# Top-k threshold search: 12 bits on VectorE and 20 on ScalarE, in place of 16 and 16

## What is computed

```python
dots = jnp.einsum('bqhd,bsd->bqhs', iqb, ik) * idx_scale
score = jnp.einsum('bqh,bqhs->bqs', iwb * w_scale, jax.nn.relu(dots))
score = jnp.where(admissible[None], score.astype(jnp.float32), -jnp.inf)
_, sel = lax.top_k(score, k_sel)          # k_sel = 256
...
logits = jnp.where(valid[:, :, None, :], logits, -jnp.inf)
p = jax.nn.softmax(logits, axis=-1).astype(c.dtype)
return jnp.einsum('bqhk,bqkr->bqhr', p, c_sel)
```

## Time and profile before

| | |
|---|---|
| median of 3 runs | 5240.14 us (5222.53 to 5248.61) |
| profiled execution | 5238.8 us, its span 5237.1 us |
| busy: PE | 4364.4 us (83%) |
| busy: DVE | 2653.6 us (51%) |
| busy: ACT | 1922.6 us (37%) |
| busy: POOL | 715.8 us (14%) |
| TensorE clock granted, mean | 0.827 |

### The profile page before, as it was taken

How to read it: one execution, slowest core, us unless ns; L and a number is a source line. 1 busy time by engine, 2 the same in 40 slices (tenths; PEclk the granted TensorE clock), 3 DMA queues, 4 the chain that set the end, 5 groups by cost and what they waited for, 6 DMA issues and landing times. The chain is left out here.

```text
span 5237.1 us, 65208 instructions
## 1 busy us (share of the span) xinstructions
PE 4364.4 (83%) x23554; PEld 3243.7 (62%) x23554; DVE 2653.6 (51%) x5390; ACT 1922.6 (37%) x3900; POOL 715.8 (14%) x745
## 2 busy tenths in 40 slices
PE   7997999983588888888898999977778878787679
PEld 6876777772466665566787888853344445454467
DVE  3113444454555544444212111138888888888545
ACT  3112332333323332333101101023677776777621
POOL 3102111100000000000000000003222333344410
PEclk9998999985567777768899999976677788778789
DMA  5327665653000000000433212120000000101033
GB/s 182 118 111 242 208 220 203 214 199 130 28 24 24 24 24 24 12 23 3 147 114 113 85 65 81 55 71 17 23 32 19 19 19 19 37 19 35 31 125 117
DMA packets 203393, 425.84 MB, mean 81 GB/s; under 512 B 37224, under 2 KB 67596, under 8 KB 202908
## 3 DMA queue, kind: packets, MB, share of 16 engines
q1 hardware_dynamic: 203072, 421.67, 23.4%
HBM read 299.93 MB, written 121.65 MB: 80 GB/s over the span
## 5 line engine op out<-in xcount | busy, mean ns | idle before, releaser
L3151 POOL TENSOR_TENSOR ds_E<-ds_bT 128x256 f32<-128x256 f32 x112 | 72.4, 647 | 2843.4 <-ACT ds_bT L3120 2660.3
L2684 PE MATMUL ds_big<-ds_ikT,ds_iqT 64*128 64x512 f32 (+3 forms) x608 | 390.9, 772 | 79.3 <-ACT ds_iqT L2661 56.7
L301 PE MATMUL g_acc<-g_ws_hi,g_hT_hi 128*128 128x512 f32 (+1 forms) x1024 | 386.8, 378 | 0.0
L303 PE MATMUL g_acc<-g_ws_hi,g_hT_lo 128*128 128x512 f32 (+1 forms) x1024 | 385.2, 376 | 0.0
L302 PE MATMUL g_acc<-g_ws_lo,g_hT_hi 128*128 128x512 f32 (+1 forms) x1024 | 385.2, 376 | 0.0
L529 PE MATMUL mm_big<-mm_gw_hi,mm_ghT_hi 128*128 128x512 f32 (+1 forms) x768 | 319.2, 416 | 31.6 <-PEq L134 31.2
L2738 DVE TENSOR_SCALAR_CACHE_REDUCE ds_eq<-ds_hi,ds_num 128x2048 uint16<-128x2048 uint16 (+13 forms) x224 | 331.3, 1479 | 25.8 <-issue 3.7
L531 PE MATMUL mm_big<-mm_gw_hi,mm_ghT_lo 128*128 128x512 f32 (+1 forms) x768 | 301.0, 392 | 0.0
L530 PE MATMUL mm_big<-mm_gw_lo,mm_ghT_hi 128*128 128x512 f32 (+1 forms) x768 | 299.8, 390 | 0.0
L2778 ACT ACTIVATE ds_signs<-ds_lo,ds_at 128x2048 bf16<-128x2048 uint16 (+13 forms) x224 | 291.3, 1301 | 1.5
L328 DVE COPY g_stage<-g_acc 128x512 f32<-128x512 f32 (+1 forms) x64 | 41.5, 649 | 459.2 <-PE g_acc L303 459.2
(11 more groups left out here) (520 smaller groups left out, 10172.9 us busy)
## 6 DMA issues: line engine op xcount, KB each, us to landing
mm_ghT_hi<-turned SPq DMA_DIRECT2D x96, 512.0 KB, 4.2
mm_ghT_lo<-turned SPq DMA_DIRECT2D x96, 512.0 KB, 5.5
proj<-g_stage SPq DMA_DIRECT2D x112, 256.0 KB, 2.0
proj<-mm_gstage SPq DMA_DIRECT2D x80, 256.0 KB, 5.0
mm_x<-proj SPq DMA_DIRECT2D x64, 256.0 KB, 3.8
second_raw<-in_w_in SPq DMA_DIRECT2D x56, 256.0 KB, 4.1
proj<-fp_stage SPq DMA_DIRECT2D x48, 256.0 KB, 2.0
mm_graw<-in_w_in SPq DMA_DIRECT2D x40, 256.0 KB, 6.3
```

Of the source, the lines that this page charges most:

```text
L301: pe.matmul(sums, hT.hi[:, k, tile], wt.hi[:, k, 0:width], start=(k == 0), stop=False)
L303: mm = pe.matmul(sums, hT.lo[:, k, tile], wt.hi[:, k, 0:width], start=False, stop=(k == KD - 1))
L2684: pe.matmul(big[:, n % 2, 0:wd], iqT[o, h // 2], b.ikT[o, x:x + wd], start=True, stop=True)\
```

## The change

The split between the two searches moves: VectorE finds the upper 12 bits (`UPPER`), ScalarE the lower 20 (`LOWER`). So each of the 14 tiles has 4 passes with their small operations less on VectorE and 4 more on ScalarE. `hi` is now the key's upper 16 bits shifted right by 4, `lo` the lower 20 bits, which no longer fit 16 bits: they are cut out with a 32-bit and, and after the closing of the upper search stand as 32-bit floats, which hold 20 bits exactly. Putting the key together takes one more small operation at L2798 and one more further on. The places move too: ScalarE's bits now run from 0.02 to 0.571, VectorE's wait for them is at 0.69 in place of 0.66, the first two passes of the mask at 0.73 and 0.77 in place of 0.7 and 0.75.

```diff
+UPPER, LOWER = 12, 20
...
-    b.lo = B.sb("lo", [P, 2, SEQ], U16)
+    b.lo = B.sb("lo", [P, 2, SEQ])
...
-        dve.tensor_copy(hi, halves[:, :, 1])
-        dve.tensor_copy(lo, halves[:, :, 0])
-        for bit in range(15, -1, -1):
-            yield 0.03 + 0.56 * (15 - bit) / 16
+        dve.tensor_scalar(hi, halves[:, :, 1], 16 - UPPER, None, ALU.logical_shift_right)
+        dve.tensor_scalar(lo.bitcast(U32), u, (1 << LOWER) - 1, None, ALU.bitwise_and)
+        for bit in range(UPPER - 1, -1, -1):
+            yield 0.03 + 0.56 * (UPPER - 1 - bit) / UPPER
...
-        dve.scalar_tensor_tensor(out=lo, in0=hi, scalar=cand, in1=lo, op0=ALU.is_equal, op1=ALU.mult)
+        dve.scalar_tensor_tensor(out=lo, in0=hi, scalar=cand, in1=lo.bitcast(U32), op0=ALU.is_equal, op1=ALU.mult)
...
-        for bit in range(15, -1, -1):
-            yield 0.02 + 0.56 * (15 - bit) / 16
+        for bit in range(LOWER - 1, -1, -1):
+            yield 0.02 + 0.58 * (LOWER - 1 - bit) / LOWER
...
-        yield 0.66
+        yield 0.69
         dve.wait_ge(s.low_found, 1)
-        dve.tensor_copy(bits.bitcast(U16)[:, 1:2], top)
-        dve.tensor_scalar(bits.bitcast(U16)[:, 0:1], at[:, 1:2], -1.0, None, ALU.mult)
+        dve.tensor_scalar(bits.bitcast(U16)[:, 1:2], top, float(1 << 16 - UPPER), None, ALU.mult)
+        dve.tensor_scalar(bits.bitcast(U16)[:, 0:1], top, 0.0, None, ALU.mult)
+        dve.tensor_scalar(below.bitcast(U32), at[:, 1:2], -1.0, None, ALU.mult)
```

More of the change, by code:

```diff
@@ L2698, in threshold_buffers @@
     b.kept = B.sb("kept", [P, 2, 3])
-    b.counts = B.sb("counts", [P, 16])
-    b.sums = B.sb("sums", [P, 16])
+    b.counts = B.sb("counts", [P, UPPER])
+    b.sums = B.sb("sums", [P, LOWER])
     b.at = B.sb("at", [P, 3])
@@ L2726, in vector @@
         yield 0.0
-        dve.memset(cand, 32768.0)
+        dve.memset(cand, float(1 << UPPER - 1))
         dve.tensor_scalar(u.bitcast(I32), score.bitcast(I32), 31, -2 ** 31, ALU.arith_shift_right, ALU.bitwise_or)
@@ L2766, in lower_half @@
     cell = lambda n: b.num[:, n:n + 1]
-    bits, sign, n_lo, want = (cell(n) for n in range(4, 8))
+    below, bits, sign, n_lo, want = (cell(n) for n in range(3, 8))
     top, need, level = (b.kept[:, k % 2, n:n + 1] for n in range(3))
@@ L2773, in scalar @@
             return
-        for bit in range(15, -1, -1):
-            yield 0.02 + 0.56 * (15 - bit) / 16
-            now, then = at[:, 2:3] if bit == 15 else at[:, bit % 2:bit % 2 + 1], at[:, 1 - bit % 2:2 - bit % 2]
+        for bit in range(LOWER - 1, -1, -1):
+            yield 0.02 + 0.58 * (LOWER - 1 - bit) / LOWER
+            now, then = at[:, 2:3] if bit == LOWER - 1 else at[:, bit % 2:bit % 2 + 1], at[:, 1 - bit % 2:2 - bit % 2]
             act.activation(signs, lo, ACT.Sign, bias=now, accum_out=sums[:, bit:bit + 1])
@@ L2806, in vector @@
         dve.tensor_scalar(sign.bitcast(I32), sign.bitcast(I32), -2 ** 31, None, ALU.bitwise_or)
+        dve.tensor_tensor(bits.bitcast(U32), bits.bitcast(U32), below.bitcast(U32), ALU.bitwise_or)
         dve.tensor_reduce(n_lo, sums[:], AX.X, ALU.max)
@@ L2811, in vector @@
         dve.drain()
-        yield 0.7
+        yield 0.73
         dve.tensor_scalar(eq, score, bits, None, ALU.is_equal)
         dve.drain()
-        yield 0.75
+        yield 0.77
         dve.tensor_tensor_scan(sel, eq, eq, 0.0, ALU.add, ALU.max)
@@ L3323, in _ @@
             dve.memset(hb.state[:], 0.0).then_inc(s.cleared, 1)
-            dve.memset(tb.at[:, 2:3], -32767.5).then_inc(s.begun, 1)
+            dve.memset(tb.at[:, 2:3], -(2.0 ** (LOWER - 1) - 0.5)).then_inc(s.begun, 1)
             dve.wait_ge(s.c_in, 16)
```

## The result

The changed kernel takes 5313.4 us (median of 4 runs, 5298.9 to 5336.1), the kernel before 5240.0. The ratio is 1.0152, with a 95% interval of 1.0121 to 1.0183: slower by 1.5%, 73 us between the medians. The forecast was 5273 us, 33 us slower, with a range up to 5305. The sign was right, the time lies above the range, and the loss is more than twice the forecast.

The account below looks back on a forecast made before the run. The prediction took each step as bound first by the longer of VectorE's and ScalarE's queues, then by VectorE. Its terms, -10 + 20 + 5.5 + 14.5 + 4 = +34 us, gave 5273 us, own range 5250 to 5295, 8-in-10 range 5235 to 5305.

Parts of the forecast that it names:

- ScalarE's queue up to its last bit sets the first part of a step: Second-layer steps: first part lasts as long as the longer of both engines' queues, the second is VectorE's; ScalarE has little room.
- The new waits for turns ahead of the closing: Sign in step 4: VectorE newly waits for ScalarE's turns before its closing copy, which comes 3 to 5 us later.
- Steps 2 to 7: Wide steps: ScalarE's turns delay VectorE's close, some 4 us in step 4; together +20 us, ends 8 and 30.
- Step 1: Step with an upper search and no lower: four VectorE bits less, 11.5 us, taken as 10 us shorter.
- the 5 us that it drew from it: By the skill's rule, step 1 would gain 5 us in place of 10, and the sum would be 5 us higher.
- The small edits: Two more small operations at the join in 14 steps, +4 us; the shift and 32-bit and taken as 0.
- Steps 8 to 11: Narrower steps with a finer margin: step 9 is 1.3 us longer, the four together +5.5 us.
- the margin taken off in the narrow steps: Step 9: VectorE's lag behind ScalarE's last bit, 4521.98 to 4528.97, absorbs most of the four bits' 8.5 us.
- Steps 12 to 15: Narrowest steps, ScalarE's last bit already last to arrive: 4, 3, 2.5 and 5 us longer, together +14.5, ends 7 and 20.
- Everything behind ScalarE slips: Rival, chance 0.10: the longer search delays TensorE's and GpSimd's chains; 5350 us at most, 5300 if only narrow steps slip.
- The draw: Rival, chance 0.28: ScalarE's waits vanish and VectorE's lag cushions, so steps 2 to 11 cost little; +13 us, 5252 us.
- VectorE's busy time: Rival, chance 0.10: VectorE's load decides each step, so most of 105 us is gained; about 5160 us.

Follow-up runs that it names:

- e2: Kernel before, with four more ScalarE search rounds whose results are not used and VectorE's 16 bits untouched: 5303.6 us, ratio 1.0137.
- e1: Kernel before, with the last four of VectorE's 16 search bits left out and ScalarE as before: 5210.6 us against 5232.4, ratio 0.9960.
- n1: Kernel before, with the attention's work (all but loads and stores) left out in steps 8 to 11: those steps took 299.2 us.
- n2: Changed kernel, with the attention's work (all but loads and stores) left out in steps 8 to 11: those steps took 320.7 us.
- e4: Changed kernel's code with the split back at 16 and 16 bits and the old places: 5237.0 us against 5232.4, ratio 1.0008.
- e8: Changed kernel with 14 bits on VectorE and 18 on ScalarE, and ScalarE's bits, VectorE's wait and the mask at later places: 5267.9 us, ratio 1.0052.
- e9: Kernel before (16 and 16 bits) with ScalarE's bits, VectorE's wait and the mask's passes at later places: 5210.4 us against 5237.3, ratio 0.9943.

## Why the forecast was right in its sign and half in its size

**ScalarE's queue up to its last bit sets the first part of a step: right in steps 2 to 7.** e2 has the loss without VectorE's part of the change, and e1 shows VectorE's bits at a fifth of their time. In step 4 the last bit came at 84.3 us into the step (84.7 forecast), VectorE's closing copy at 82.8 (77.9 before), 4.9 later where 2.6 to 5.5 were forecast, and the step took 4.4 us more (4 forecast). The new waits for turns ahead of the closing are the ones named; those for logits, which had 2.4 us before and are the longer now, were not. VectorE in step 4, from its start to its wait:

```profile
DVE ds_L L2963 <- PE ds_big L3025: 9.6, 7, 2.3
DVE ds_score L2647 <- ACT ds_rel L2668: 8.3, 6, 3.7
```

Steps 2 to 7 came to +23.2 for +20. Single steps scatter (step 5 +9.6, step 6 -1.1), and n1 and n2, with the same work in these steps, differ by 25.8, so the close agreement of this term is in part luck.

**Step 1: right.** 8.6 us shorter for 10; e1 has 7.7 there, with VectorE's bits alone. This is where the passes themselves can be priced. The Trainium skill ("ScalarE: Activation LUTs", Rules for kernel authors) sends relu, max, min, add and mul to VectorE, which it calls up to about three times faster per element in bf16. The prediction stretched this to the counting pass, and the 5 us that it drew from it are not what was measured: a pass with a count takes VectorE 2346 ns at 2048 elements and ScalarE 1993. For VectorE's plain operations this case doesn't contradict it: a shift of 1920 words takes 1.16 us (below), ScalarE's Sign over 1792 1.78. Floats are read at the pace of 16 bits. ScalarE by shape:

```profile
L2782 ACT ACTIVATE ds_signs<-ds_lo,ds_at 128x2048 bf16<-128x2048 f32 x20 | 39.9, 1993 | 0.0
```

1993 ns against 1994.

**The small edits: nothing against it.** e4 has 4 us for 4, in an interval that takes in zero. The shift of 16-bit words, which no row of before showed, costs what the copy did. VectorE at the start of step 2, beside the earlier trace rows:

```profile
3700.01 1.16 DVE L2736 TENSOR_SCALAR ds_hi<-ds_eq 128x1920 uint16<-128x1920 uint16 x1
3701.09 1.15 DVE L2737 TENSOR_SCALAR ds_lo<-ds_eq 128x1920 uint32<-128x1920 uint32 x1
```

**Steps 8 to 11: the step that failed.** For step 9 I forecast ScalarE's last bit 9.1 us later, and it came 9.8 later (58.2 to 68.0 us into the step). But I took the 7 us that VectorE needed from there to its wait as a cushion: 4532.3 - 4529.0 - 2 = 1.3 us. (The terms given there add up to 4531.8 and not 4532.3, and in step 4 the lower end of the close comes to 2.9 and not 2.6 us; neither changes the account.) Most of it was none. VectorE in step 9 before, where it was idle 0.6 us in this stretch:

```profile
4524.74 0.12 DVE L2746 COPY ds_kept<-ds_num 128x1 f32<-128x1 f32 x1
...
4528.62 0.43 DVE L2957 CUSTOM_DVE_ANT_0 ds_L<-ds_big,ds_sel 128x256 f32<-128x256 f32 x1 [0.61 <-PE ds_big L3019]
```

and with the change:

```profile
4566.02 0.42 DVE L2963 CUSTOM_DVE_ANT_0 ds_L<-ds_big,ds_sel 128x256 f32<-128x256 f32 x1 [4.79 <-PE ds_big L3025]
...
4575.30 0.14 DVE L2750 COPY ds_kept<-ds_num 128x1 f32<-128x1 f32 x1
...
4581.91 0.42 DVE L2963 CUSTOM_DVE_ANT_0 ds_L<-ds_big,ds_sel 128x256 f32<-128x256 f32 x1 [2.96 <-PE ds_big L3025]
...
4587.21 0.69 DVE L2963 CUSTOM_DVE_ANT_0 ds_L<-ds_big,ds_sel 128x512 f32<-128x512 f32 x1 [3.46 <-PE ds_big L3025]
...
4587.83 0.15 DVE L2802 TENSOR_SCALAR ds_num<-ds_kept 128x1 uint16<-128x1 f32 x1
```

and ScalarE's last bit in it:

```profile
4578.01 0.29 ACT L2786 ACTIVATE ds_at<-ds_way,ds_at 128x1 f32<-128x1 f32 x1
```

VectorE's closing copy came 4.1 us later in its step (61.0 to 65.0), less than the last bit, so up to there the cushion did give. Then it was lost again. From the start of the last bit's row to the operation behind VectorE's wait it is 9.8 us, more than the 7.3 before, and of these VectorE is idle 6.4, for logits. What stands there is work that VectorE gets only as ScalarE and TensorE hand it over, and so it moved along with ScalarE; a lighter search doesn't help, as e1 takes four bits off VectorE and gains 0.6 us in these four steps. The step took 7.9 us more.

So the step of the prediction that failed is the margin taken off in the narrow steps: in steps 8 to 11 it left 5.5 us of a queue that keeps ScalarE busy 29.4 us longer, and the runs show 28.1 (28.1 in e2 too, with VectorE's own bits untouched).

**Steps 12 to 15: the same error, smaller.** Step 15, where the margin was nil, took 5.0 us more for 5. In steps 12, 13 and 14, where I had let pieces moved ahead of the wait and VectorE's margin take something back, it was 8.5, 7.4 and 7.4 for 4, 3 and 2.5. I had said that VectorE would wait 2 to 6 us a step at its wait for the last bit. In steps 12 to 15 these waits are 0.8 us in all, so for step 15 the number was right and the wait was not the one named. VectorE waited earlier, 38.0 us for logits. Its wait for the last bit:

```profile
DVE ds_num L2802 <- ACT ds_at L2786: 0.8, 1, 0.8
```

**The rivals.** "Everything behind ScalarE slips" came true in the narrow steps, in the form that the prediction called half of it, and its 5300 us lie in the range, 13 us below the time; it had 0.10. Its condition was read too narrowly: I asked for waits of VectorE behind its wait for the lower search, and they came ahead of it. The draw and VectorE's busy time fell with the result, and e2 shows why.

**Still open.** How the loss in steps 2 to 7 is divided between the turns (14.6 to 58.1 us of waits) and the logits (15.0 to 43.1); why 14 and 18 at late places is slow there (e8); whether other places are better still than e9's, and which of the moved places it is; and what costs steps 12 to 15 so much, where VectorE and ScalarE are both idle over a quarter of the time before the change. TensorE is also slower at its work: its busy time over steps 1 to 15 grew from 1098.1 to 1133.7 us with the same matmuls, at a granted clock of 0.73 to 0.76 in place of 0.76 to 0.78 in steps 2 to 15. What of this lies on the path was not tried.

## What to carry to other kernels

A lag between an engine's last result and the moment when its neighbour takes it is a cushion only if the neighbour spends it on a backlog of its own; take the work off the neighbour (one run) and see whether the time moves, before you count on it. Where two engines arrive close together, either one alone, relieved, gains a little, and the same work added costs more (here -22 and -35 us for four bits less, +71 for four more), so a shift between them can lose though its parts look balanced. And where an engine in strict order serves others, the places of the long work can matter as much as its amount: later places gave 27 us at no work saved, while no other split tried was faster than 16 and 16 at the same places.

## What was not expected of the hardware

For the pass that counts, ScalarE is the faster engine in wide tiles, and they meet in narrow ones: VectorE's pass over 16-bit words takes 2346 ns at 2048 elements and 612 at 384, ScalarE's Sign with its sum 1993 and 608, over 32-bit floats as over 16-bit words. Beside the pass a bit costs ScalarE 191 ns to read the sum and twice 295 ns for operations on one column; VectorE reads its count in 83 ns and does its two in 154 and 216 (247 before). In the changed kernel's trace TensorE did the same matmuls at a granted clock lower by 0.02 to 0.04 in the stretches in which it stood longer for ScalarE. Such a wait might so be paid a second time, but the runs don't agree on it: in e2, with a like loss, its busy time grew from 457.7 to 472.0 us in steps 8 to 15, and in steps 2 to 7 it was 556.0 us against 556.6 although TensorE waited 34.2 us for the copies in place of 15.8. How much of this reaches the end was not tried.
